# Second attention of a fused two-block kernel in 24 steps in place of 32: the tiles of 128 and 256 keys of a head pair share a step

## What is computed

```
    qkv = h @ w_qkv
    q, k, v = jnp.split(qkv, 3, axis=-1)
    q = head_rmsnorm(q.reshape(B, S, N_HEADS, HEAD_DIM), q_norm)
    k = head_rmsnorm(k.reshape(B, S, N_HEADS, HEAD_DIM), k_norm)
...
        s = jnp.einsum('bqhd,bkhd->bhqk', qc, kb).astype(jnp.float32) * scale + bias[None]
        s = jnp.where(valid[None, None, None, :], s, -1e30)
        p = jax.nn.softmax(s, axis=-1).astype(vb.dtype)
        return jnp.einsum('bhqk,bkhd->bqhd', p, vb)
...
    return o @ w_o
```

## Time and profile before

| what | value |
|---|---|
| median of 3 runs | 1681.31 us |
| the profiled execution | 1680.72 us, of which the span of the profile is 1678.8 us |
| TensorE busy | 1659.2 us, 99% of the span |
| VectorE, ScalarE, GpSimd busy | 56%, 37%, 5% |
| DMA | 92 GB/s over the span |
| second attention, first scores to last values product | 1112.9 to 1289.9 us |

### The profile page before, as it was taken

The page is one execution under the profiler, slowest core; times in us unless marked ns, Lnnn a source line. Parts: engine busy times, 40 slices in busy tenths (PEclk is TensorE's granted clock), DMA queues, the critical chain, the costliest instruction groups (busy, mean ns, idle before and its releaser), DMA issues.

```text
span 1678.8 us, 19277 instructions
## 1 busy us (share of the span) xinstructions
PE 1659.2 (99%) x8138; PEld 1343.9 (80%) x8138; DVE 943.8 (56%) x1426; ACT 618.4 (37%) x867; POOL 83.7 (5%) x81
## 2 busy tenths in 40 slices
PE   9979999999999999999999999999999999999999
PEld 7857778888888888888888888877767888888887
DVE  6677865534343556667556456555655577366453
ACT  5456533423231335533223223445554433122220
POOL 1200000000000000000000000311100200000000
PEclk9989999999999999999999999999999999999999
DMA  5210226535363522223322222312221223322321
GB/s 182 103 47 25 77 101 101 134 80 112 103 112 104 118 81 75 76 76 116 110 100 101 100 77 99 125 54 96 88 86 51 74 89 114 100 85 92 108 75 69
DMA packets 27622, 155.94 MB, mean 93 GB/s; under 512 B 3664, under 2 KB 4832, under 8 KB 11664
## 3 DMA queue, kind: packets, MB, share of 16 engines
q1 hardware_dynamic: 26064, 149.84, 25.2%
q0 software_dynamic: 1328, 4.86, 5.1%
q10 hardware_dynamic: 144, 0.00, 0.0%
HBM read 149.98 MB, written 4.72 MB: 92 GB/s over the span
## 4 chain that ended last, share of the span: by engine, by line
PE 95%; DVE 4%; ACT 1%; DMA 0%; issue 0%; POOL 0%; SPq 0%; DVEq 0%; ACTq 0%
PE bank L536 26%; PE bank L538 25%; PE bank L537 25%; PE bank L542 3%; PE bank L544 3%; PE bank L543 3%; PE bank L1131 1%; PE bank L1153 1%; PE bank L1140 1%; PE bank L751 1%; DVE WL L1577 1%; PE bank L797 1%; PE bank L706 0%; PE bank L772 0%; PE bank L1119 0%; DVE AT L1830 0%
## 5 line engine op out<-in xcount | busy, mean ns | idle before, releaser
L536 PE MATMUL bank<-AH,WH 128*128 128x512 f32 (+1 forms) x1152 | 453.1, 393 | 3.1 <-DVE X L2099 1.8
L538 PE MATMUL bank<-AH,WL 128*128 128x512 f32 (+1 forms) x1152 | 449.1, 390 | 0.0
L537 PE MATMUL bank<-AL,WH 128*128 128x512 f32 (+1 forms) x1152 | 448.9, 390 | 0.0
L1577 DVE TENSOR_TENSOR WL<-RAW,WH 128x2048 fp32r<-128x2048 f32 (+1 forms) x133 | 298.5, 2247 | 178.5 <-ACT WH L1198 178.5
L1198 ACT ACTIVATE WH<-RAW 128x2048 fp32r<-128x2048 f32 (+1 forms) x133 | 248.4, 1871 | 257.5 <-PE bank L538 238.9
L536 PEld LDWEIGHTS bank<-AH,WH 128*128 128x128 f32 (+1 forms) x1152 | 216.0, 187 | 50.7 <-issue 4.2
L538 PEld LDWEIGHTS bank<-AH,WL 128*128 128x128 f32 (+1 forms) x1152 | 215.9, 187 | 46.1
L537 PEld LDWEIGHTS bank<-AL,WH 128*128 128x128 f32 (+1 forms) x1152 | 216.0, 188 | 45.1 <-issue 1.0
L536 PE MATMUL bank<-HH,WH 128*128 128x512 f32 x608 | 239.9, 395 | 0.0
L538 PE MATMUL bank<-HH,WL 128*128 128x512 f32 x608 | 238.4, 392 | 0.0
L537 PE MATMUL bank<-HL,WH 128*128 128x512 f32 x608 | 236.3, 389 | 0.0
(11 more groups left out here) (291 smaller groups left out, 1771.6 us busy)
## 6 DMA issues: line engine op xcount, KB each, us to landing
RAW<-in_W SPq DMA_DIRECT2D x124, 1024.0 KB, 4.8
RAW<-in_W SPq DMA_DIRECT2D x9, 768.0 KB, 4.1
X<-in_XT SPq DMA_DIRECT2D x16, 256.0 KB, 3.8
ev_scratch<-ev POOLq DMA_DIRECT2D x16, 160.0 KB, 7.6
Gb<-ev_scratch SPq DMA_DIRECT2D x16, 128.0 KB, 3.3
out<-X SPq DMA_DIRECT2D x8, 256.0 KB, 2.0
Gb<-ev_scratch SPq DMA_DIRECT2D x16, 112.0 KB, 2.7
RAW<-in_W SPq DMA_DIRECT2D x3, 512.0 KB, 6.1
```

What stands on the lines that cost most here:

```text
L536: e.matmul(o, a, h, start=first, stop=False)
L537: e.matmul(o, a, l, start=False, stop=False)
L538: return e.matmul(o, c, h, start=False, stop=last)
L1577: e.tensor_tensor(k.WL[j][:, 0:n], k.RAW[RAW_OF[u]][:, 0:n], k.WH[j][:, 0:n].bitcast(F), SUB).then_inc(*WLO.mark(u))
```

## The change

A step is now an entry of a list `ATTEND`: each head pair has three, the tiles (0, 1) together, then tile 2, then tile 3. The tile of 128 keys takes columns 0 to 127 of the bank and of `pb2`, the tile of 256 keys columns 128 to 383. Every per-tile operation on scores, exponentials and products stays, one for each tile. What is done once per step (reciprocal, ScalarE's copy of the turned weights, the semaphore waits) is done once for both tiles. The list has 24 steps and 27 turns; the 28 groups stand in turns 0 to 14, the 16 parts in turns 15 to 26, one or two in a turn.

```
+ATTEND = [(p, qs) for p in range(8) for qs in ((0, 1), (2,), (3,))]
+
+def pieces(u):
+    return [(j, q, P * (q == 1), (q + 1) * P) for j, q in enumerate(ATTEND[u][1])]
+
+def width(u):
+    return sum(n for _, _, _, n in pieces(u))
...
-    steps, last = 32, 18
+    steps, last = len(ATTEND), 14
+    parts, tail = [(m, i) for m in range(8) for i in range(2)], steps + 2 - last
...
-            m, i = divmod(s - last - 1, 2)
-            project(m, i)
-            if i == 0 and m > 0:
-                out.append(("add", m - 1))
+            for m, i in parts[16 * (s - last - 1) // tail:16 * (s - last) // tail]:
+                project(m, i)
+                if i == 0 and m > 0:
+                    out.append(("add", m - 1))
...  TensorE, "scores" (after the waits)
-                e.matmul(bank[3 + hh][:, 0:n], k.qTa[rows, p, q * P:(q + 1) * P], k.kTa[rows, p, 0:n], start=True,
-                         stop=True).then_inc(*MM.mark("s2", i, hh))
+            for _, q, at, n in pieces(i):
+                for hh in range(2):
+                    rows = slice(64 * hh, 64 * hh + 64)
+                    t = e.matmul(bank[3 + hh][:, at:at + n], k.qTa[rows, p, q * P:(q + 1) * P], k.kTa[rows, p, 0:n], start=True,
+                                 stop=True, skip_group_check=True)
+                    if q == qs[-1]:
+                        t.then_inc(*MM.mark("s2", i, hh))
...  TensorE, "turned"
-                for c in range(q + 1):
+                for c in range(width(u) // P):
...  ScalarE, "weights"
-                e.activation(k.pb2[y][:, 0:n], k.pb2[y][:, 0:n], AF.Exp, bias=k.st2[:, y, 0:1], scale=-1.0,
-                             accum_out=k.st2[:, y, 2:3]).then_inc(*ACT.mark("p2", i, hh))
+                for j, _, at, n in pieces(i):
+                    t = e.activation(k.pb2[y][:, at:at + n], k.pb2[y][:, at:at + n], AF.Exp, bias=k.st2[:, y, j, 0:1], scale=-1.0,
+                                     accum_out=k.st2[:, y, j, 2:3])
+                t.then_inc(*ACT.mark("p2", i, hh))
...  VectorE, "norm"
+            e.reciprocal(k.st2[:, y:y + 2, 0:m, 3], k.st2[:, y:y + 2, 0:m, 2]).then_inc(*DVE.mark("inv2", i))
+            w.wait_ge(DVE("inv2", i))
+            for hh in range(2):
+                z = k.pb2[y + hh]
+                for j, _, at, n in pieces(i):
+                    t = e.tensor_scalar(z[:, at:at + n], z[:, at:at + n], k.st2[:, y + hh, j, 3:4], None, MUL)
+                t.then_inc(*DVE.mark("pn2", i, hh))
```

More of the change, by code:

```diff
@@ L279, in memory @@
     k.Gb = [a.tile(f"Gb{i}", [P, 512]) for i in range(4)]
-    k.st2 = a.tile("st2", [P, 6, 4])
+    k.st2 = a.tile("st2", [P, 6, 2, 4])
     k.pb2 = [k.rb, k.acc] + [a.tile(f"pb2{i}", [P, 512]) for i in range(4)]
@@ L482, in attend_order @@
             out.append(("values", s - 3))
-            if (s - 3) % NT == 3:
-                out.append(("output", (s - 3) // NT))
+            p, qs = ATTEND[s - 3]
+            if qs[-1] == 3:
+                out.append(("output", p))
         if s < steps:
@@ L1123, in tensor_program @@
             i, = x
-            p, q = divmod(i, NT)
-            n = (q + 1) * P
-            w.wait_ge(*(ACT("zt", blk, t) for blk in (p // 4, 2 + p // 4) for t in range(q + 1)))
+            p, qs = ATTEND[i]
+            w.wait_ge(*(ACT("zt", blk, t) for blk in (p // 4, 2 + p // 4) for t in range(qs[-1] + 1)))
             for hh in range(2):
                 w.wait_ge(*free[3 + hh])
-            for hh in range(2):
-                rows = slice(64 * hh, 64 * hh + 64)
-                e.matmul(bank[3 + hh][:, 0:n], k.qTa[rows, p, q * P:(q + 1) * P], k.kTa[rows, p, 0:n], start=True,
-                         stop=True).then_inc(*MM.mark("s2", i, hh))
-                free[3 + hh] = [DVE("s2", i, hh)]
+            for _, q, at, n in pieces(i):
[5 more added lines that the diff above has]
+                        t.then_inc(*MM.mark("s2", i, hh))
+                        free[3 + hh] = [DVE("s2", i, hh)]
         elif step == "turned":
             u, = x
-            p, q = divmod(u, NT)
             for hh in range(2):
                 w.wait_ge(DVE("pn2", u, hh), *free[5 + hh])
-                for c in range(q + 1):
+                for c in range(width(u) // P):
                     t = e.transpose(bank[5 + hh][:, c * P:(c + 1) * P], k.pb2[2 * (u % 3) + hh][:, c * P:(c + 1) * P], ident)
@@ L1144, in tensor_program @@
             u, = x
-            p, q = divmod(u, NT)
+            p, qs = ATTEND[u]
             b = 2 if p >= 4 and p % 2 == 0 else 7
-            if q == 0:
+            if qs[0] == 0:
                 w.wait_ge(ACT("v2", 4 + p // 4, 3), *free[b])
[L1149 to L1157, removed]
+            for hh in range(2):
+                w.wait_ge(ACT("pt2", u, hh))
+            for _, q, at, n in pieces(u):
+                for c in range(q + 1):
+                    for hh in range(2):
+                        h, y = 2 * p + hh, 2 * (u % 2) + hh
+                        t = e.matmul(bank[b][64 * hh:64 * hh + 64, q * P:(q + 1) * P], k.v2[:, c, h * 64:(h + 1) * 64],
+                                     ptb[y][:, at + c * P:at + (c + 1) * P], start=c == 0, stop=c == q, skip_group_check=True)
+                        if c == q == qs[-1]:
+                            t.then_inc(*MM.mark("o2", u, hh))
+            if qs[-1] == 3:
                 k.where["o2", p] = b
@@ L1300, in scalar_program, with turned_weights @@
     ptb = t2s + sq
-    def turned_weights(name, b, u, hh):
-        x, q = 2 * (u % 2) + hh, u % NT
+    def turned_weights(name, b, u, n, hh):
+        x = 2 * (u % 2) + hh
         w.wait_ge(MM(f"t{name}", u, hh))
@@ L1306, in turned_weights @@
             w.wait_ge(MM(f"o{name}", u - 2, hh))
-        e.activation(ptb[x][:, 0:(q + 1) * P], bank[b + hh][:, 0:(q + 1) * P], AF.Copy).then_inc(*ACT.mark(f"pt{name}", u, hh))
+        e.activation(ptb[x][:, 0:n], bank[b + hh][:, 0:n], AF.Copy).then_inc(*ACT.mark(f"pt{name}", u, hh))
     def head(x, g):
@@ L1334, in scalar_program @@
             for hh in range(2):
-                turned_weights("1", 4, u, hh)
+                turned_weights("1", 4, u, (u % NT + 1) * P, hh)
         if i < 3 * NT:
@@ L1540, in scalar_program @@
             i, = x
-            n = (i % NT + 1) * P
             for hh in range(2):
@@ L1544, in scalar_program @@
                 w.wait_ge(DVE("s2", i, hh))
-                e.activation(k.pb2[y][:, 0:n], k.pb2[y][:, 0:n], AF.Exp, bias=k.st2[:, y, 0:1], scale=-1.0,
-                             accum_out=k.st2[:, y, 2:3]).then_inc(*ACT.mark("p2", i, hh))
+                for j, _, at, n in pieces(i):
+                    t = e.activation(k.pb2[y][:, at:at + n], k.pb2[y][:, at:at + n], AF.Exp, bias=k.st2[:, y, j, 0:1], scale=-1.0,
+                                     accum_out=k.st2[:, y, j, 2:3])
+                t.then_inc(*ACT.mark("p2", i, hh))
         elif step == "turned":
             for hh in range(2):
-                turned_weights("2", 5, *x, hh)
+                turned_weights("2", 5, *x, width(*x), hh)
         elif step == "output":
             p, = x
-            w.wait_ge(MM("o2", 4 * p + 3, 1))
+            w.wait_ge(MM("o2", 3 * p + 2, 1))
             e.activation(k.OH[p][:, :], bank[k.where["o2", p]][:, :], AF.Copy).then_inc(*ACT.mark("oh2", p))
@@ L1872, in chain, with divided @@
             t.then_inc(*DVE.mark("state", j, c))
[L1874 to L1879, removed]
+    def divided(i, n):
+        y, st = 2 * (i % 3), k.st1
+        w.wait_ge(ACT("p1", i, 1))
+        e.reciprocal(st[:, y:y + 2, 3], st[:, y:y + 2, 2]).then_inc(*DVE.mark("inv1", i))
+        w.wait_ge(DVE("inv1", i))
         for hh in range(2):
             e.tensor_scalar(pb[y + hh][:, 0:n], pb[y + hh][:, 0:n], st[:, y + hh, 3:4], None, MUL).then_inc(
-                *DVE.mark("pn" + name, i, hh))
+                *DVE.mark("pn1", i, hh))
     zeros = cst[:, C_ZERO:C_ZERO + 1]
@@ L1897, in vector_program @@
         if 0 <= u < 4 * NT:
-            divided("1", u, (u % NT + 1) * P, k.st1, pb)
+            divided(u, (u % NT + 1) * P)
         if i < 4 * NT:
@@ L2181, in vector_program @@
             i, = x
-            n = (i % NT + 1) * P
             for hh in range(2):
-                h, y = 2 * (i // NT) + hh, 2 * (i % 3) + hh
+                h, y = 2 * ATTEND[i][0] + hh, 2 * (i % 3) + hh
                 w.wait_ge(MM("s2", i, hh), (k.gb_in[h % 4], 32 * (h // 4 + 1)), POOL("r4", 5))
@@ L2187, in vector_program @@
                     w.wait_ge(MM("t2", i - 3, hh), DVE("pn2", i - 3, hh))
-                e.tensor_tensor_reduce(out=k.pb2[y][:, 0:n], in0=bank[3 + hh][:, 0:n], in1=k.Gb[h % 4][:, 512 - n:512], scale=-0.125,
-                                       scalar=3.0e38, op0=ADD, op1=MIN, accum_out=k.st2[:, y, 0:1]).then_inc(*DVE.mark("s2", i, hh))
+                for j, _, at, n in pieces(i):
+                    t = e.tensor_tensor_reduce(out=k.pb2[y][:, at:at + n], in0=bank[3 + hh][:, at:at + n],
```

(20 more changed lines are left out.)

## The result

The changed kernel takes **1674.43 us** (median of 5, 1673.95 to 1676.65) against 1681.31 us of before (median of 5). The ratio is 0.9964 with a 95% interval of 0.9953 to 0.9974: faster by 0.36%. The forecast was 1674.8 us.

A forecast was written before the change was run, and what follows sets the result against it. TensorE, busy 1659.2 of 1678.8 us, was taken as the bound. 5.7 us from fewer shape changes plus 0.9 us of wait gave 6.6 us less: forecast 1674.8 us, range 1673.8 to 1676.0 (69%), 8 in 10 within 1673.6 to 1677.6.

The forecast's parts named there:

- One turn of the loop pays 0.21 + 0.15 + 0.15 + 0.20 = 0.71 us that buy nothing: TensorE's attention turns: fixed costs at changes of weight shape; each of four changes falls by 8, saving 5.7 us.
- The second pair of scores pays nothing: Scores of two tiles side by side on TensorE pay the fixed 0.21 us once: 0.85 us instead of 1.05.
- the first rival: Fixed cost of scores is per pair, not per shape change: 4.0 us go, 1676.4 to 1677.3 us; chance 12%.
- The wait of 0.90 us goes: TensorE's wait at 1185.89, 128-key scores waiting for VectorE to read the bank, most likely goes: 0.90 us taken.
- 0.5 us to spare: Turn 7, single qkv group: ScalarE, VectorE and GpSimd chain 8.5 us against 9.0 us of TensorE work.
- VectorE and ScalarE: price 0, covered by the turns: Fewer reciprocals and copies gain nothing; the shared step's longer loop, 4.6 against 4.05 us, hides under TensorE's turns.
- the slower rival: Score banks become the bound: shared step's reduces come late behind 512-key turns, 1687.6 us; chance 5%.
- The stretch "170.4 us": Attention from first scores to last values product was to fall from 177.0 to 170.4 us.

## Why the prediction was right, point by point

- **"One turn of the loop pays 0.21 + 0.15 + 0.15 + 0.20 = 0.71 us that buy nothing", 8 times less: 5.7 us.** Shown. The like-for-like stretch fell by 8.1 - 1.4 = 6.7 us (176.7 to 168.6, less one part), 5.7 and 0.9 with 0.1 left. In the forecast of the total the 0.1 us from 1674.7 to 1674.8 have no term. That the cost goes with the change of shape, not with a run, a wait or the step count, is shown by other orders of the same instructions: 0.80 to 0.66 us for the transposes when they follow large products, 1.4 us more when two pairs of scores are set apart, the same entry prices when scores and values products trade places.
- **The second pair of scores pays nothing.** Shown: 0.86 us, the first rival wanted 1.05. By the rule of the Trainium skill, page "TensorEngine Tiling (Array Packing)", Key Properties (a change of mode drains, a change of tile doesn't), that is what was to come; the trace agrees, and adds the price, 0.15 to 0.21 us. That the array drains in this time is the page's reading; no row shows it. What the rows do show is the weight load (PEld):

```profile
1248.89 0.19 PEld L550 LDWEIGHTS bank<-OH,WH 128*128 128x128 f32 x1 [0.17 <-issue]
1248.89 0.50 PE L550 MATMUL bank<-OH,WH 128*128 128x512 f32 x1
...
1248.99 0.19 PEld L551 LDWEIGHTS bank<-OL,WH 128*128 128x128 f32 x1
...
1249.23 0.40 PE L551 MATMUL bank<-OL,WH 128*128 128x512 f32 x1
```

  At the change (L550) the load starts together with its matmul; inside the run (L551) it starts 0.24 us ahead, under the matmul before. And the loads last 0.19 us for scores, 0.14 for transposes, 0.14 for values products and 0.19 for large products (medians in the changed kernel), close to the prices 0.21, 0.15, 0.15 and 0.20. So the price may be in the main a weight load that nothing hides. No run varied the load by itself, so this is a reading.
- **The wait of 0.90 us goes.** It went, and by moving one group in either kernel it goes or comes back alone. But I gave turn 7 of the changed kernel 0.5 us to spare, and nothing was left. The chain there, and the timeline's rows of the weight load of these scores and of the copy of group 31:

```profile
1170.85 0.44 PE bank L1133 x4
1171.29 1.10 PE bank L1145 x4
```

```profile
1163.23 0.67 ACT L1545 ACTIVATE qn<-bank,r 128x512 f32<-128x512 f32 x1
...
1171.23 0.33 PEld L1145 LDWEIGHTS bank<-kTa,qTa 64*128 64x128 f32 x4 [0.18 <-DVE st L2206]
```

  These scores cost 1.10 us, the other seven of 512 keys 1.06 each: they came 0.04 us late, so the margin was mis-sized by 0.54 us. On TensorE's side I had charged group 32 with 0.20 us for a change of shape, though it stands right behind group 31 and took 2.72 us, not 2.96. On the other side copy, square and sums took 2.9 us, not 2.3: group 31 ended at 1162.50, but ScalarE was in the exponentials of a shared step and began the copy at 1163.23. That all but 0.04 us of a wait stayed away in this turn was in part luck: the reserve that I had counted on was not there.
- **VectorE and ScalarE: price 0, covered by the turns.** Shown from both sides. With the parts in place TensorE is busy for all of the 53.4 us of their turns; without that cover the loops cost 10.3 us. The loop of a whole pair, 11.5 to 11.7 us, against 14.2 us of TensorE's turns (4.05 + 4.27 + 4.48 + 1.38) is the distance that this change kept from the slower rival. In the turns with groups the cover was as thin as the point above says.
- **The stretch "170.4 us".** The figure was wrong by its own terms: I had not counted that two parts now stand behind the last values products. The windows gave 168.8, and 168.8 + 1.38 = 170.2 is the quantity that I had worked out. The total time doesn't hang on it.

## What to carry to other kernels

Read the chain in order of time, not busy time, and fit a line through runs of different length on TensorE: what doesn't scale is paid at each change between full, 64-row and 64-column matmuls, here 0.15 to 0.21 us each, invisible in a TensorE that is "99% busy". Before merging steps, see whether an order with fewer changes exists: putting the full-shape transposes next to the full-shape products gained 0.15 us a turn in either kernel, and on top of the merge it is, level with the order that has the values products ahead of the scores, the fastest version here (1671.7 and 1671.6 us). And merge only as far as the work between hides the longer loop; its length can be added up from durations (11.6 expected, 11.52 and 11.66 measured). A lower clock on an engine that would have waited anyway costs next to nothing (0.14 us for a pair at 0.85), so compare whole periods before counting it as a loss.

## What was not expected of the hardware

The executions of most of these kernels fall into two groups some 2 us apart (1674.0 to 1674.4 and 1676.5 to 1676.7 for the changed one). The traces put much of it ahead of the second attention. In the first block TensorE waits 9.1 us for VectorE, until 103.7 us, and around this wait the granted clock is lower. The windows of two executions, the changed kernel and then the kernel before with one group moved:

```profile
100.00:120.00 20.00, 15.95 (x78) 11.97 (x80) 13.23 (x36) 12.12 (x27) 1.80 (x1) 0.80 0.06 25
```

```profile
100.00:120.00 20.00, 15.95 (x69) 12.75 (x70) 12.56 (x32) 11.51 (x25) 1.80 (x1) 0.68 0.06 27
```

The clock is 0.80 in the one and 0.68 in the other, and in the 20 us ahead 0.95 and 0.98. Together the second execution had (0.12 - 0.03) x 20 = 1.8 us less of full clock, at most that much time, and the second attention begins at 1113.3 and at 1115.4 us. A second dip comes later, and not always. From 200 to 220 us the clock is 0.91 in the changed kernel and 1.00 in the version with the values first:

```profile
200.00:220.00 20.00, 20.00 (x146) 17.47 (x145) 10.74 (x16) 8.91 (x11) 1.64 (x1) 0.91 0.20 61
```

```profile
200.00:220.00 20.00, 20.00 (x159) 17.78 (x158) 10.73 (x16) 9.02 (x11) 1.64 (x1) 1.00 0.19 61
```

There the second attention begins at 1111.9 us. Nothing differs in what the programs do up to there, so a gain of 1 us is read from the stretch that it belongs to, not from the span. Why the clock stays down for longer in some executions, and why the second dip is missing in one, these runs don't tell.
